# A product of zeros at the end of each slot of PE, and a tile's v sum taken ahead of the next c

## The chip, the cores and the metric

The kernel runs on one core of a Trainium2 chip. The metric is the device time of one launch in microseconds (us). The engines are named as in the profile: PE multiplies matrices, DVE, ACT and POOL work on vectors, SP issues transfers. POOL issues the gathers of table rows here.

## What is computed

One layer of a decoder for 1024 tokens of width 1024: an input norm and projection, an RWKV-7 recurrence and a causal convolution side by side, gates and an output projection, then the part that moves most of the data, a feed-forward layer of single experts, a gate from a per-layer embedding, and a last norm.

```python
h = h + (g_r * o_r + g_c * o_c) @ w_out              # RWKV-7 and convolution, gated
c = rms_norm(h, norm_ffn_g)
# peer_ffn(c): 8 heads, 16 experts each = 128 selections for a token
idx, gates = top_k_product_keys(c @ w_q, sub_keys)    # 128 of 16384 experts
u = jnp.take(u_tab, ib, axis=0)                       # 128 rows of 1024 for each token
coef = gb * gelu(einsum('cd,ced->ce', xb, u))
h = h + einsum('ce,ced->cd', coef, jnp.take(v_tab, ib, axis=0))
h = h + sigmoid(rms_norm(h, ple_norm_g) @ ple_w_gate) * (p @ ple_w_proj)
return rms_norm(h, final_norm_g)
```

Each token reads 128 rows of u and 128 rows of v, 4 KB each: 1.07 GB in all.

## The kernel before

**Tiles, periods, slots.** The tokens are cut into 8 tiles of 128 (NT = 8). After a start phase the program runs periods t = 0 to 10 of 128 slots s each, on every engine in the same written order, held together by semaphores alone. A period works on three tiles at once:

- The u part of tile t. In slot s POOL gathers row s of all 128 tokens' selections (gather_u, L761, 512 KB) into a ring of five buffers (UR = 5), and DVE takes 128 dot products of it with c (dot, L1924). The gather into a buffer waits for the dot that used it last.
- The v part of tile t - 2 (LAG = 2). In slot s POOL gathers the 128 rows of one token (gather_v, L778, 512 KB) into a ring of six buffers (VR = 6), ahead of that slot's gather_u in the same queue. PE multiplies these rows with the token's coefficients (add_tokens, L1085).
- The mixers of tile t + 1 (front), laid out over the slots on PE, ACT and DVE. Slots 20 to 66 hold the recurrence: 30 steps, one each 1.5 slots, in each of which a small product of PE (L803, L816, L825, L830, L872 to L889) waits for a copy of ACT (L1213) or an operation of DVE (L1553 to L1571) that waits for the product before. Slots 74 to 88 hold the mixers' products (L908), slots 90 to 97 the output projection (L983), slots 104 to 115 the queries (L1001).

In periods 0 and 1 there is no v part; PE has the projection of the later tokens instead (L1155). In period 7 there is no front. Periods 8 and 9 have v parts only, four tokens at a time, with eleven buffers.

**A token's v product.** The accumulator acc is 128 x 1024 in PSUM and is seen as four strips of 32 rows. Weights are 128 x 32 (the coefficients of one token in one of 32 columns, zeros beside), so a product writes one strip. Slot j's first half of columns goes to strip j % 4, its second half to strip (j % 4) ^ 2; products on different strips can run beside each other. Each float32 product stands in the trace as two matmuls, so a slot's two products are four records, "x4". A product with start=False adds to what the strip holds. The last product of slot j raises s_vmm, for which gather_v of token j + 6 waits.

**The end of a tile.** summed (L1933) adds acc to the residual hh with three DVE operations. It waits for all 128 tokens of the tile (s_vmm), and PE's first product of the next tile waits for it (s_hh), since it overwrites acc. It stands behind the second dot of the period. make_c (L1818) makes the period's c from the front's results and stands ahead of the first dot; the dots wait for it.

**Names.** e_v, e_u, e_a_rstd: ring buffers (e_a_rstd is the fifth of the u ring); e_wd: weights of the v products; e_acc: the accumulator; e_arena, e_pd: the recurrence's operands and its PSUM; e_zero: a tile of zeros that ACT spreads between the weights (spread); e_ones: a tile of ones; e_hh: the residual; e_gbc, e_hc, e_cw: the convolution.

Of the kernel before, what the change touches and what calls it, by code (L numbers as in the profile page):

```python
# [17 lines left out]
P = 128  # L18
# [278 lines left out]
def tail_step(t, s):  # L297

    if t == NT - 1:
        m, k = divmod(s - TAIL_AT, TAIL_SPAN)  # L300
        return (m, k) if 0 <= m < EARLY_TAILS else None
    if NT <= t < NT + LAG and 10 <= s < 10 + TAIL_SPAN:
        return EARLY_TAILS + t - NT, s - 10
    if t == NT + LAG and s < TAIL_SPAN:
        return NT - 1, s
    return None


def trunk(nc, io, dram):

    with ExitStack() as ctx:
        def buf(name, shape, dt=F32):
            return ctx.enter_context(nc.sbuf_tensor(name, shape, dt))
# [89 lines left out]
        pick = buf("e_pick", [P, 2, TOPK])  # L403
        iot, ioti = buf("e_iota", [P, TOPK]), buf("e_iotai", [P, TOPK], mybir.dt.int32)
        ex, ssum = buf("e_exp", [P, PH, TOPK]), buf("e_ssum", [P, PH])
        zero = buf("e_zero", [P, QUARTER * LANES])
        idx = [buf(f"e_idx{i}", [P, NSEL], U32) for i in range(2)]
        fidx = buf("e_idxf", [P, NSEL])
        idxT = [buf(f"e_idxT{i}", [P, P], U32) for i in range(LAG + 1)]
# [381 lines left out]
        def _(pe):  # L791
# [273 lines left out]
            def add_tokens(n, j, together):  # L1065
# [8 lines left out]
                for h in range(D // HALF):  # L1074
# [3 lines left out]
                    for i in range(together):  # L1078
# [8 lines left out]
                        if h == D // HALF - 1:  # L1087
                            last.then_inc(s_vmm, 1)

            def front(n, s):  # L1090
                if s in (2, 5, 9):
                    prep(n, (2, 5, 9).index(s))
                r = rec_step(s)
                if r:
                    rec(2 * n + r[0], r[1])
                if s == MIX_AT:
                    conv_mean(n)
                if s == MIX_AT + 1:
                    y_mean(n)
                if s == MIX_AT + 2:  # L1100
                    conv_variance(n)
                if s == MIX_AT + 3:
                    y_variance(n)
                for k in range(2 * KT):
                    if s == product_slot(k):
                        (conv_product, y_product)[k // KT](n, k % KT)
                if MIX_AT + 24 <= s < MIX_AT + 24 + KT:
                    mixed(n, s - MIX_AT - 24)
                if s == MIX_AT + 35:
                    c_turned(n)  # L1110
                if MIX_AT + 38 <= s < MIX_AT + 38 + FIRST_HEADS:
                    queries(n, s - MIX_AT - 38)
                if s == MIX_AT + 41:
                    scores(n, 0)
                if MIX_AT + 42 <= s < MIX_AT + 42 + PH - FIRST_HEADS:
                    queries(n, (4, 5, 6, 7, 2, 3)[s - MIX_AT - 42])
                if s == NEXT_HEAD_AT + HEAD_SPAN - 4:
                    scores(n, 1)
# [41 lines left out]
            def tail(m, k):  # L1160
                if k == 1:
                    tail_turned(m)
                if 4 <= k < 4 + KT:
                    ple_gate(m, k - 4)
                if k == 13:
                    ple_proj(m)
# [18 lines left out]
            for t in range(NT + LAG + 1):  # L1185
                for s in range(SLOTS):
                    if t < BLOCKS:
                        for i in behind_products(t, s):
                            behind_product(t, i)
                    if 1 <= t <= NT and s == 8:  # L1190
                        coef_turned(t - 1)
                    if LAG <= t < NT + LAG:
                        together = LAST_TOGETHER if t >= NT else TOGETHER
                        if s % together == 0:
                            add_tokens(t - LAG, s, together)
                    if t < NT:
                        for h in range(2, PH):
                            if s == head_slot(h) - 4:
                                scores(t, h)
                        if s == HEADS_END + 2:  # L1200
                            indices_turned(t)
                    if t + 1 < NT:
                        front(t + 1, s)
                    if tail_step(t, s):
                        tail(*tail_step(t, s))

        @block.scalar
        def _(act):
# [208 lines left out]
            def places(q):  # L1417
                w = wd[q % 2][:, :].rearrange("p (i x) -> p i x", x=WROW)
                q %= NSEL // (QUARTER * LANES)
                return w[:, :, QUARTER * q:QUARTER * q + 32 * (LANES - 1) + 1:32]  # L1420

            def spread(n, q):
                if n * (NSEL // (QUARTER * LANES)) + q >= 2:
                    act.wait_ge(s_vmm, n * NSEL + (q - 1) * QUARTER * LANES)
                act.activation(places(q + 6), zero[:, :].rearrange("p (i g) -> p i g", g=LANES), ACT.Copy)
                act.wait_ge(s_coT, n + 1)
                act.activation(places(q), coefT[n % 2][:, :].rearrange("p (g s) -> p s g", g=LANES)[:, QUARTER * q:QUARTER * (q + 1), :],
                               ACT.Copy).then_inc(s_wd, 1)
# [107 lines left out]
        def _(dve):  # L1536
# [486 lines left out]
            for s in range(FRONT_SLOTS, SLOTS):  # L2023
                front(0, s)
            for t in range(NT + LAG + 1):
                if t < NT:
                    make_c(t)
                for s in range(SLOTS):
                    if t < NT:
                        dot(t, s)  # L2030
                        if 0 <= s - head_slot(1) - 8 < 6:
                            select(t, 1, s - head_slot(1) - 8)
                        if s < head_slot(1) + 8:
                            head(t, 1, s - head_slot(1))
                    if s == (1 if t < NT + LAG else 0) and t > LAG:
                        summed(t - LAG - 1)
                    if s == 3 and 1 <= t <= NT:
                        coefficients(t - 1)
                    if t < NT:
                        for h in range(2, PH):  # L2040
                            if head_slot(h) <= s < head_slot(h) + 8:
                                head(t, h, s - head_slot(h))
                            if head_slot(h) + 8 <= s < head_slot(h) + 14:
                                select(t, h, s - head_slot(h) - 8)
                        if s == HEADS_END:
                            less_max(t)
                            indices_out(t)
                        if s == HEADS_END + 4:
                            softmax(t)
                            token_indices(t)  # L2050
                    if t < BLOCKS and s:
                        for m in behind_done(t, s - 1):
                            if kind(m) in ("z", "conv"):
                                behind_out(t, m)
                    if t + 1 < NT:
                        front(t + 1, s)
                    if tail_step(t, s):
                        tail(*tail_step(t, s))
# [71 lines left out]
```

## Time and profile before

| | |
|---|---|
| median of 3 runs | 3707.59 us (3706.16 to 3715.51) |
| the profiled execution | 3706.03 us, span 3704.3 us |
| mean granted clock of PE | 0.841 of full |
| PE, DVE, ACT, POOL busy | 2755.3, 2368.4, 525.3, 1979.5 us |
| make_c (L1818) of tiles 0 to 7 starts at | 276.8, 609.5, 945.9, 1346.3, 1741.6, 2126.9, 2522.7, 2914.3 us |
| summed (L1933) of tiles 0 to 7 starts at | 1351.9, 1747.3, 2132.5, 2529.1, 2919.4, 3283.5, 3479.0, 3666.4 us |

The starts of make_c mark the periods. Periods 0 and 1 take 333 and 336 us, periods 2 to 6 take 400, 395, 385, 396 and 392 us, period 7 takes 369 us, periods 8 and 9 some 190 us each.

### The profile page before, as it was taken

To read this page: it belongs to the slowest core of one execution; us is meant where nothing else is said; L and a number is where in the kernel's file an instruction comes from. 1 tells how busy PE (TensorE), PEld (TensorE's weight loads), DVE (VectorE), ACT (ScalarE), POOL (GpSimd) and SP (SyncE) were. 2 spreads that over 40 slices of the span, in tenths; PEclk is the share of its full clock that TensorE was granted. 3 is DMA by queue.
4 is the path that set the end of the run, shared out by engine and by line. 5 is a ranking of instruction groups with operands and counts; after the bars stand their busy time and mean duration, and the time that the engine had idled before them with its cause. 6 is when DMAs were issued, how large, how long until landed. Compare 5 with 4: busy or idle time off the path is not lost.

```text
span 3704.3 us, 41438 instructions
## 1 busy us (share of the span) xinstructions
PE 2755.3 (74%) x15264; PEld 1272.2 (34%) x15264; DVE 2368.4 (64%) x6063; ACT 525.3 (14%) x1165; POOL 1979.5 (53%) x2093
## 2 busy tenths in 40 slices
PE   9988988998657766676567756775667777677877
PEld 7764655556233322332133213331333112111111
DVE  4549889888767677676867686768675665520000
ACT  3222112221101010111110011101110121110000
POOL 0003334334556666566656665666566666656663
PEclk9999999999767877787778867886788778779999
DMA  6538899889999999999999999999999999999995
GB/s 194 178 133 278 295 319 344 284 285 333 355 323 345 404 378 360 335 394 370 367 334 396 380 366 333 383 382 385 331 362 402 409 388 373 379 372 356 373 354 207
DMA packets 381194, 1253.76 MB, mean 338 GB/s; under 512 B 40384, under 2 KB 76480, under 8 KB 380224
## 3 DMA queue, kind: packets, MB, share of 16 engines
q0 software_dynamic: 294912, 1073.87, 77.6%
q1 hardware_dynamic: 83776, 176.20, 13.4%
q8 instruction: 120, 1.97, 0.2%
q10 hardware_dynamic: 2304, 1.05, 0.1%
q14 instruction: 82, 0.67, 0.0%
HBM read 1221.47 MB, written 29.49 MB: 338 GB/s over the span
## 4 chain that ended last, share of the span: by engine, by line
PE 19%; DVE 18%; another core or an unknown queue 15%; issue 11%; DMA 10%; POOL 8%; ACT 2%; SPq 0%; POOLq 0%; DVEq 0%; ACTq 0%
DVE e_u L1924 6%; PE e_acc L1085 6%; DMA e_v<-in_v_tab,e_idxT 5%; POOL e_v L778 4%; DMA e_u<-in_u_tab,e_idx 3%; PE e_pd L983 2%; PE e_acc L1155 2%; POOL e_u L761 2%; DVE e_gbc L1659 2%; PE e_pd L1001 2%; PE e_pd L803 2%; DVE e_a_rstd L1924 2%; PE e_pd L1054 2%; PE e_pd L908 1%
## 5 line engine op out<-in xcount | busy, mean ns | idle before, releaser
L1085 PE MATMUL e_acc<-e_v,e_wd 128*32 128x512 f32 x3636 | 1079.2, 762 | 397.8 <-DMA e_v<-in_v_tab,e_idxT 269.2
L761 POOL DMA_INDIRECT e_u<-in_u_tab,e_idx x820 | 797.2, 972 | 863.2 <-DVE e_dots L1924 412.8
L1924 DVE CUSTOM_DVE_ANT_0 e_u<-e_u,e_c 128x1024 f32<-128x1024 f32 x820 | 996.0, 1215 | 311.5 <-DMA e_u<-in_u_tab,e_idx 251.7
L778 POOL DMA_INDIRECT e_v<-in_v_tab,e_idxT x909 | 866.0, 953 | 613.2 <-issue 220.4
L1085 PEld LDWEIGHTS e_acc<-e_v,e_wd 128*32 128x32 f32 x3636 | 145.0, 120 | 976.4 <-DMA e_v<-in_v_tab,e_idxT 581.1
L1155 PE MATMUL e_acc<-e_v 128*128 128x384 f32 x1216 | 434.3, 501 | 24.7 <-DMA e_v<-in_w_in 16.6
L1659 DVE SCALAR_TENSOR_TENSOR e_gbc<-e_hc,e_cw,e_gbc 128x128 f32<-128x128 f32 x960 | 310.4, 344 | 1.9 <-issue 0.6
L1924 DVE CUSTOM_DVE_ANT_0 e_a_rstd<-e_a_rstd,e_c 128x1024 f32<-128x1024 f32 x204 | 247.8, 1215 | 73.4 <-DMA e_a_rstd<-in_u_tab,e_idx 63.1
L803 PE MATMUL e_pd<-e_arena 64*64 64x64 f32 x3584 | 168.8, 251 | 159.8 <-ACT e_arena L1213 70.8
L1155 PEld LDWEIGHTS e_acc<-e_v 128*128 128x128 f32 x1216 | 224.7, 193 | 178.2 <-issue 28.6
L761 POOL DMA_INDIRECT e_a_rstd<-in_u_tab,e_idx x204 | 198.3, 972 | 130.8 <-DVE e_dots L1924 87.7
L803 PEld LDWEIGHTS e_pd<-e_arena 64*64 64x64 f32 x3584 | 144.2, 160 | 306.6 <-issue 129.6
L1933 DVE TENSOR_TENSOR e_hh<-e_hh,e_acc 64x512 f32<-64x512 f32 (+1 forms) x24 | 16.4, 683 | 275.2 <-remote 139.5
L1213 ACT ACTIVATE e_arena<-e_pd 128x512 f32<-128x512 f32 (+1 forms) x192 | 90.4, 471 | 708.8 <-remote 345.4
L983 PE MATMUL e_pd<-e_w_out,e_actT 128*128 128x512 f32 x256 | 138.2, 671 | 35.4 <-DVE e_actT L1790 26.7
L1001 PE MATMUL e_pd<-e_actT,e_w_q 128*128 128x128 f32 x1024 | 143.6, 296 | 17.0 <-issue 8.7
L1001 PEld LDWEIGHTS e_pd<-e_actT,e_w_q 128*128 128x128 f32 x1024 | 133.0, 208 | 63.0 <-issue 48.4
L1129 PE MATMUL e_acc<-e_w_q,e_u 128*128 128x256 f32 x608 | 141.5, 386 | 3.4 <-DVE e_w_q L2008 3.4
L1085 PE MATMUL e_acc<-e_u,e_wd 128*32 128x512 f32 x368 | 121.7, 629 | 25.3 <-DMA e_u<-in_v_tab,e_idxT 16.2
L1054 PE MATMUL e_pd<-e_w_out,e_actT 128*128 128x512 f32 x256 | 125.8, 625 | 2.3 <-ACT e_actT L1261 2.3
L1129 PEld LDWEIGHTS e_acc<-e_w_q,e_u 128*128 128x128 f32 x608 | 114.5, 192 | 23.2 <-issue 5.2
L778 POOL DMA_INDIRECT e_u<-in_v_tab,e_idxT x92 | 86.7, 943 | 48.9 <-issue 23.7
(266 smaller groups left out, 2761.1 us busy)
## 6 DMA issues: line engine op xcount, KB each, us to landing
e_v<-in_w_in SPq DMA_DIRECT2D x76, 512.0 KB
e_u<-in_w_in SPq DMA_DIRECT2D x38, 512.0 KB, 3.7
e_v<-in_v_tab,e_idxT POOLq DMA_INDIRECT x909
e_u<-in_u_tab,e_idx POOLq DMA_INDIRECT x820
e_ring<-in_w_c SPq DMA_DIRECT2D x32, 256.0 KB
e_zb<-in_w_c SPq DMA_DIRECT2D x32, 256.0 KB
e_ring<-in_w_r SPq DMA_DIRECT2D x32, 256.0 KB
e_zb<-in_w_r SPq DMA_DIRECT2D x32, 256.0 KB
```

Source lines behind the costliest of these rows:

```text
L761: pool.indirect_dma_start(out=u[m % UR][:, :], out_offset=None, in_=io["u_tab"], in_offset=bass.IndirectOffsetOnAxis(ap=idx[n % 2][:, j:j ...
L778: pool.indirect_dma_start(out=v[i], out_offset=None, in_=io["v_tab"], in_offset=bass.IndirectOffsetOnAxis(ap=idxT[n % (LAG + 1)][:, k:k + ...
L803: last = pe.matmul(pi[r, out, i * CH:(i + 1) * CH], a[r, i, :], b[r, i, :] if len(b.shape) == 3 else b[r, :], start=True, stop=True)
L983: last = pe.matmul(pd[:, h * HALF:(h + 1) * HALF], mixt[:, k, :], w_out[:, k, h * HALF:(h + 1) * HALF], start=(k == 0), stop=(k == KT - 1))
L1001: last = pe.matmul(pd[:, h * P:(h + 1) * P], w_q[:, k, h * P:(h + 1) * P], actT[:, k, :], start=(k == 0), stop=(k == KT - 1))
L1054: last = pe.matmul(pd[:, h * HALF:(h + 1) * HALF], actT[:, k, :], w_ple[:, k, h * HALF:(h + 1) * HALF], start=(k == 0), stop=(k == KT - 1))
L1085: last = pe.matmul(acc[rows, cols], w[:, at_:at_ + 32], v[v_place(m)[0]][:, cols], start=(step == 0), stop=True, skip_group_check=True)
L1129: last = pe.matmul(out, w_a[m % UW][:, k, :], ahead[:, k, :], start=(k == 0), stop=(k == KT - 1))
L1155: last = pe.matmul(acc[:, m % 2 * HALF:m % 2 * HALF + BEHIND_T], w_b[m % 2][:, k, :], behind[:, k, :], start=(k == 0), stop=(k == KT - 1))
L1213: act.activation(dst, src, ACT.Copy).then_inc(s_ra, 1)
L1659: dve.scalar_tensor_tensor(out=out, in0=hc[:, i, j:j + P], scalar=col(cw, j * CONV_TILES + i), in1=out, op0=ALU.mult, op1=ALU.add).then_in ...
L1924: dve.tensor_tensor_reduce(u[m % UR][:, :], u[m % UR][:, :], c[:, :], 1.0, 0.0, ALU.mult, ALU.add, dots[n % 2][:, j:j + 1]).then_inc(s_dot, 1)
```

## The change

Three things. keep_warm(s), a new function on PE, multiplies 32 columns of zeros with 512 columns of ones and adds the product to the strip s % 4, first half of columns, of acc. It runs as the last thing of slots 4 to 126 in periods 2 to 7: 738 times. It waits for nothing and raises nothing. The tile of zeros grows from 16 to 32 columns. And summed of the tile that is done moves on DVE from behind the second dot of a period to ahead of make_c.

```diff
-        zero = buf("e_zero", [P, QUARTER * LANES])
+        zero = buf("e_zero", [P, 32])
...
+            def keep_warm(j):
+                rows = slice(32 * (j % LANES), 32 * (j % LANES) + 32)
+                pe.matmul(acc[rows, 0:HALF], zero[:, :], ones[:, :].unsqueeze(1).to_broadcast([P, HALF // P, P]), start=False,
+                          stop=True, skip_group_check=True)
...
                     if tail_step(t, s):
                         tail(*tail_step(t, s))
+                    if LAG <= t < NT and LANES <= s < SLOTS - 1:
+                        keep_warm(s)
...
-                act.activation(places(q + 6), zero[:, :].rearrange("p (i g) -> p i g", g=LANES), ACT.Copy)
+                act.activation(places(q + 6), zero[:, 0:QUARTER * LANES].rearrange("p (i g) -> p i g", g=LANES), ACT.Copy)
...
             for t in range(NT + LAG + 1):
+                if t > LAG:
+                    summed(t - LAG - 1)
                 if t < NT:
                     make_c(t)
                 for s in range(SLOTS):
...
-                    if s == (1 if t < NT + LAG else 0) and t > LAG:
-                        summed(t - LAG - 1)
```

On PE, in the recurrence of a tile, the program stands in this order before (L803 a step of the recurrence, L1085 the v products, x4 or more where two or more slots follow each other with nothing between them; here one product is one row):

```order
L1085 MATMUL e_acc<-e_v,e_wd 32x512 x2
L803 MATMUL e_pd<-e_arena 64x64 x16
L1085 MATMUL e_acc<-e_v,e_wd 32x512 x4
L803 MATMUL e_pd<-e_arena 64x64 x8
L803 MATMUL e_pd<-e_m_id,e_arena 64x64 x8
L1085 MATMUL e_acc<-e_v,e_wd 32x512 x2
```

and now, the same stretch, with the new product as L1092:

```order
L1085 MATMUL e_acc<-e_v,e_wd 32x512 x2
L803 MATMUL e_pd<-e_arena 64x64 x16
L1092 MATMUL e_acc<-e_ones,e_zero 32x512
L1085 MATMUL e_acc<-e_v,e_wd 32x512 x2
L1092 MATMUL e_acc<-e_ones,e_zero 32x512
L1085 MATMUL e_acc<-e_v,e_wd 32x512 x2
L803 MATMUL e_pd<-e_arena 64x64 x8
L803 MATMUL e_pd<-e_m_id,e_arena 64x64 x8
L1092 MATMUL e_acc<-e_ones,e_zero 32x512
L1085 MATMUL e_acc<-e_v,e_wd 32x512 x2
```

Each slot's v products are followed by the slot's own other work and then by one product of zeros; where two slots' v products followed each other, a product of zeros now stands between them.

On DVE, at the start of a period, before (L1818 is make_c, L1924 a dot, L1933 the sum):

```order
L1849 MAX e_best<-e_onehot 128x8
L1818 SCALAR_TENSOR_TENSOR e_c<-e_x,e_stats,e_gt 128x1024
L1924 ISA e_u,e_dots<-e_u,e_c 128x1024
L1924 ISA e_dots 128x1
L1852 MAX_INDEX e_pos<-e_best,e_onehot 128x8
L1853 MATCH_REPLACE e_onehot<-e_best,e_onehot 128x256
L1597 TENSOR_TENSOR e_actT<-e_arena,e_vec 128x512
L1659 SCALAR_TENSOR_TENSOR e_gbc<-e_hc,e_cw,e_gbc 128x128
L1924 ISA e_u,e_dots<-e_u,e_c 128x1024
L1924 ISA e_dots 128x1
L1856 MAX e_best<-e_onehot 128x8
L1933 TENSOR_TENSOR e_hh<-e_hh,e_acc 128x512
```

and now (all lines of DVE stand 7 further on: L1825 is make_c, L1931 a dot, L1940 the sum):

```order
L1856 MAX e_best<-e_onehot 128x8
L1940 TENSOR_TENSOR e_hh<-e_hh,e_acc 128x512
L1940 TENSOR_TENSOR e_hh<-e_hh,e_acc 64x512 x2
L1825 SCALAR_TENSOR_TENSOR e_c<-e_x,e_stats,e_gt 128x1024
L1931 ISA e_u,e_dots<-e_u,e_c 128x1024
```

The three additions stand ahead of make_c and of the period's first dot.

## Rows read from the trace of the kernel before

**Rows 1.** The page: busy time, and PE's granted clock in 40 slices.

```profile
span 3704.3 us, 41438 instructions
PE 2755.3 (74%) x15264; PEld 1272.2 (34%) x15264; DVE 2368.4 (64%) x6063; ACT 525.3 (14%) x1165; POOL 1979.5 (53%) x2093
...
PEclk9999999999767877787778867886788778779999
```

**Rows 2.** Periods 1, 2, 5, 7: each engine's busy us, clock, DMA share, GB/s.

```profile
610.00:945.00 335.00, 299.06 (x1720) 188.88 (x1721) 286.91 (x744) 75.31 (x153) 119.62 (x124) 0.95 0.88 304
```

```profile
946.00:1346.00 400.00, 267.57 (x1626) 115.04 (x1626) 282.60 (x730) 45.08 (x104) 250.12 (x262) 0.76 0.97 361
...
2127.00:2523.00 396.00, 260.57 (x1626) 110.27 (x1626) 285.19 (x734) 44.22 (x101) 252.37 (x262) 0.78 0.98 367
...
2914.00:3284.00 370.00, 263.98 (x778) 64.45 (x778) 224.72 (x517) 52.11 (x114) 242.47 (x256) 0.77 0.99 382
```

**Rows 3.** The recurrence's stretches in periods 2 to 6, same columns.

```profile
1009.00:1171.00 162.00, 102.24 (x948) 50.89 (x944) 109.46 (x302) 16.41 (x40) 95.36 (x101) 0.71 0.92 330
...
2575.00:2733.00 158.00, 99.72 (x954) 46.93 (x951) 109.27 (x300) 16.42 (x40) 94.73 (x101) 0.75 0.95 343
sum 799.00, PE 502.03 PEld 242.73 DVE 545.71 ACT 81.84 POOL 476.81; mean PE 100.41 PEld 48.55 DVE 109.14 ACT 16.37 POOL 95.36
```

**Rows 4.** Two windows behind the recurrence, same columns.

```profile
1952.00:2003.00 51.00, 39.28 (x188) 19.75 (x188) 41.63 (x105) 7.22 (x13) 33.54 (x35) 0.84 1.02 391
```

```profile
2003.00:2027.00 24.00, 16.55 (x65) 6.38 (x64) 17.64 (x40) 0.00 (x0) 15.06 (x16) 0.78 1.03 409
```

**Rows 5.** Waits of 957 to 2914 us: total us, times, longest us.

```profile
PEld e_acc L1085 <- DMA e_v<-in_v_tab,e_idxT: 341.2, 146, 7.2
ACT e_arena L1213 <- remote: 339.1, 47, 15.0
...
DVE e_u L1924 <- DMA e_u<-in_u_tab,e_idx: 170.6, 142, 12.3
...
POOL e_v L778 <- PE e_acc L1085: 145.1, 102, 5.2
...
PE e_acc L1085 <- DVE e_hh L1933: 46.6, 4, 15.0
```

**Rows 6.** The same view of 277 to 945 us.

```profile
ACT e_arena L1213 <- remote: 6.3, 1, 6.3
```

**Rows 7.** PE in the recurrence of period 4: start, us, group, idle before and releaser.

```profile
1826.45 1.79 PE L803 MATMUL e_pd<-e_arena 64*64 64x64 f32 x32 [4.23 <-ACT e_arena L1213]
1828.17 1.92 PE L1085 MATMUL e_acc<-e_v,e_wd 128*32 128x512 f32 x4
1832.50 1.15 PE L803 MATMUL e_pd<-e_arena 64*64 64x64 f32 x32 [2.40 <-ACT e_arena L1213]
1833.58 1.94 PE L1085 MATMUL e_acc<-e_v,e_wd 128*32 128x512 f32 x8
```

**Rows 8.** PE in the output projection of period 5.

```profile
2437.60 1.05 PE L1085 MATMUL e_acc<-e_v,e_wd 128*32 128x512 f32 x4
2438.59 1.98 PE L983 MATMUL e_pd<-e_w_out,e_actT 128*128 128x512 f32 x4
2440.50 1.92 PE L1085 MATMUL e_acc<-e_v,e_wd 128*32 128x512 f32 x16
```

**Rows 9.** The change from period 4 to 5 on DVE.

```profile
2126.90 1.27 DVE L1818 SCALAR_TENSOR_TENSOR e_c<-e_x,e_stats,e_gt 128x1024 f32<-128x1024 f32 x1
...
2132.49 2.10 DVE L1933 TENSOR_TENSOR e_hh<-e_hh,e_acc 128x512 f32<-128x512 f32 x3
```

**Rows 10.** The same change of periods on PE.

```profile
2122.02 1.85 PE L1085 MATMUL e_acc<-e_v,e_wd 128*32 128x512 f32 x4 [0.64 <-DMA e_v<-in_v_tab,e_idxT]
2133.26 4.60 PE L1085 MATMUL e_acc<-e_v,e_wd 128*32 128x512 f32 x12 [9.39 <-DVE e_hh L1933]
```

## The prediction, made before the changed kernel was run

> **What bounds the kernel now.** I read the page first. No engine is full: PE is busy 74% of the span, DVE 64%, and PE's clock falls from full to seven or eight tenths once the slices of periods 0 and 1 are over [rows 1]. Then the windows by period: the DMA engines are busy 0.97 to 0.99 of the time in periods 2 to 7, at 361 to 382 GB/s [rows 2]. So the gathers nearly fill a full period. Windows inside a period show two kinds of stretch. Behind the recurrence the DMA moves 391 and 409 GB/s [rows 4], and I take 409 for the most it can do. In the recurrence (five stretches, 799 us in all) it moves only 330 to 343, mean some 338 [rows 3]. There something else sets the pace, and only there can a period still gain much: at 409 GB/s the same bytes would take 799 x 338/409 = 660 us, so 139 us is the most that all five could give.
>
> What sets the pace there is in the waits. PE's v products wait for rows of v, DVE's dots for rows of u, but POOL also waits 145.1 us for PE's v products to free buffers, and ACT waits 339.1 us for something that the view can't name ("remote"), up to 15.0 us at a time [rows 5]; in periods 0 and 1 that wait is 6.3 us [rows 6]. PE's program is in order. A step of the recurrence waits for ACT or DVE, and the v products behind it wait with it; then the ring of v stays full, POOL stands at gather_v, and gather_u behind it starves DVE. The timeline shows it: PE stands 4.23 and 2.40 us for ACT's copy, with the next slots' v products behind [rows 7].
>
> PE's clock has a part in this. In the stretches it is 0.71 to 0.75 [rows 3], that is, more than half of the work at the lower level of 1.2 GHz. A step of 32 products takes 1.79 us there and 1.15 at the upper level, one slot's v products 1.92 [rows 7] against 1.05 [rows 8]. In periods 0 and 1, where PE always has a product to do, the clock is 0.95 [rows 2].
>
> **The product of zeros.** It adds 738 products to PE, 123 in each of periods 2 to 7. Nothing of this form is in the trace. The nearest is half a slot's v products: the two halves lie on different strips, run beside each other and end after 1.05 us at full clock, 1.92 at half [rows 7, 8]. One product alone then holds its strip about as long as the pair: from 0.86 us (1.92 less 1.05 is the time that a second turn on the same strips adds [rows 8]) to 1.92. Where the next slot's v product follows at once it goes to other strips and may run beside it; where PE is idle anyway it costs nothing. It costs where the slot's own v product stands directly ahead of it with the strip still taken, and something is queued behind.
>
> Its gain is the clock. PE would have one more product in each slot of three us, mostly in the idle time after the slot's v products. Take period 4, 41 us from 1816: the groups of PE that stand ahead of or in a step of the recurrence and ran at half clock exceed their length at full clock by 0.6 to 0.9 us each (1.79 against 1.15, 1.92 against 1.05 [rows 7, 8]), and I count some six of them, 4.7 us. On a stretch of 160 us that is 18 us. Against it stand the new products that end up ahead of a step that is already released, 0.86 us each, some four in a stretch: 3 us. From the remaining 15 I take off 6, because the clock won't be full throughout and because part of the steps wait for ACT and DVE, whose operations don't get faster. Term: **9 us in each of five stretches, -45 us.** Bounds: 0 if the chain waits for other things, -139 by the DMA.
>
> Outside the recurrence I cost it at nothing. In the output projection PE is full at full clock, 2.9 us a slot [rows 8], but there the new product stands behind a product that goes to another accumulator, so it may run beside the next v products; the eight slots would cost at most 8 x 0.86 = 7 us a period, if it may not. In the remaining slots the DMA is at 391 to 409 GB/s [rows 4] and PE waits for v; a faster PE changes nothing. Period 7 has 382 GB/s already [rows 2].
>
> The Trainium skill ("TensorE: Matmul & The Clock Gate", Part 1) says that the array's clock is passed in two levels and that the gate follows how busy the array has been; of zeros as operands it says nothing there. Rows 2 and 3 agree as far as they go (0.95 with a busy PE, 0.71 to 0.78 with a waiting one); that a product of zeros on one strip of four counts, no row shows. By that rule the clock comes up, and the forecast stands; without it the third rival below holds.
>
> **The sum ahead of c.** DVE does the same three additions, 2.10 us, but before make_c and not 5.59 us later (2132.49 less 2126.90 [rows 9]). PE's first v product of the next tile waits for it: at this boundary PE was done at 2123.9 and began again at 2133.26, 9.39 us idle [rows 10]. This happens at five boundaries, 46.6 us in four of the waits [rows 5]. Meanwhile all six buffers of v are full, POOL stands at gather_v, and so the DMA. The sum now starts when DVE gets there, some 5.5 us sooner, and PE with it; c and the dots start 2.1 us later, which delays the release of u buffers by as much. The end of the wait moves from gather_v to the dots, but the u ring holds five gathers. Per boundary between +2 (only the delay counts) and -5.5 us (all of it counts); I take -3, since the DMA has some gathers of u in flight meanwhile. PE was done well before DVE comes to the sum, so the wait for s_vmm, which now stands ahead of make_c and every dot, ends at once. Term: **5 x -3 = -15 us.** (Bounds -27 and +10.) The larger tile of zeros costs nothing: ACT reads the same 16 columns.
>
> **Sum.** The profiled execution took 3706.0 us (span 3704.3), 1.6 below the median. 3706 - 45 - 15 = **3646 us**.
>
> **Rivals.**
>
> *A: only the move counts.* The clock rises, but the steps of the recurrence don't come sooner, since they wait for what ACT and DVE do and for signals that arrive late: ACT's unnamed waits of 339.1 us, 47 in five periods, against 6.3 in one [rows 5, 6]. For it: ACT is busy only 14% of the span, so it is not its work that is late, and a PE product whose record has long ended is what the copy waits for; a faster product shortens no such delay. Against it: half-clock groups do stand directly ahead of steps [rows 7]. Time: 3706 - 15 = 3691, and 3695 with a smaller gain by the move.
>
> *B: slower, by PE's turn in the catch-up.* After a wait of the chain PE has two to four slots of v products queued and does them side by side: two slots in 1.94 us [rows 7], four in 1.92 at full clock [rows 8], 0.48 each. Now a product of zeros stands between each two of them, on a strip that the one ahead of it still holds: 0.86 us more a slot. The catch-up is what frees the ring of v, for which POOL waits [rows 5]; if POOL starts 0.86 us later at each, the DMA loses it. In period 4's stretch I count 13 groups of two slots or more, some 16 such pairs a period: 5 x 16 x 0.86 = 69 us. It decides when PE's catch-up and not the chain's waits holds the gathers, that is, from the point where POOL's waits for L1085 grow beyond 145.1 us. Time: 3706 + 69 = 3775.
>
> *C: the change doesn't do what it says.* A product of zeros with one strip of 32 rows doesn't lift the clock. Then each costs up to 1.92 us at half clock [rows 7]: at rival B's 80 places 154 us, and with the move's 15 off 3706 + 139 = 3845 at most. With six tenths of it on the path, 3706 + 92 - 15 = 3783; I take some 3790.
>
> **How the numbers follow.** Forecast (the chain shortens with the clock): 0.40, 3610 to 3685. A: 0.21, 3685 to 3700. B: 0.33, 3715 to 3790, thinner in the first part. C: 0.06. What a measurement of this kernel can tell from no change is 0.3%, 11 us: 3696.5 to 3718.7. Faster is the forecast and most of A (the part of it where the move gives its full 15): 0.40 + 0.09 = 0.49. Same: the rest of A, and the lower rim of B: 0.12 + 0.04 = 0.16. Slower: 0.29 + 0.06 = 0.35. The range goes from the forecast's lower part to past B's middle, 3590 to 3785, leaving out C, the last third of B and a gain beyond 116 us by the unused DMA time: some 0.18 together. The forecast's own range is 3610 to 3685.
>
> **What would show it.** Clock: the granted clock in the five stretches above 0.9, and 32 products of L803 near 1.15 us, and one slot's v products near 1.05. If it stays at 0.71 to 0.75, C. Chain: the five stretches together at 755 us and 355 GB/s; if they stay at 799 with a high clock, A. Move: the idle time of PE at the five boundaries near 5 us in place of 9.39 and up to 15.0, and the wait of L1085 for the sum near 20 us in place of 46.6; the dots' wait for u at the start of a period not up by more than the 2 us. B would show as groups of v products and products of zeros that follow each other at 0.86 us or more, POOL's wait for L1085 above 145.1 us, and GB/s below 391 behind the recurrence. I would be wrong as well if the DMA, with both rings served better, moves less than 409 GB/s at its best, since then less than 139 us was ever to be had; and if the additions wait for the last v product of the tile, which would hold make_c and all dots behind it.

## The result

The changed kernel takes 3724.36 us (median of 9 runs, 3721.08 to 3732.32), the kernel before beside it 3707.59 us (9 runs, 3700.96 to 3715.72). The ratio is 1.0036, with a 95% interval of 1.0023 to 1.0048: slower by some 13 us by the ratio (17 us by the medians), where 61 us faster was forecast. The time lies in the range; the sign is wrong. Times and ratios here leave out three executions in a slower state, one of e12 and two of e16.

### The profile page after: what moved, and what is told of

It is laid out like the page before. It is cut to its first block, busy times and chain, and to the rows that moved or that the text cites. A ratio compares the mean times of both kernels' runs of the same rounds, so it can differ in the third digit from the quotient of the medians.

```text
span 3721.0 us, 44390 instructions
## 1 busy us (share of the span) xinstructions
PE 2899.6 (78%) x16740; PEld 1317.9 (35%) x16740; DVE 2365.9 (64%) x6063; ACT 526.1 (14%) x1165; POOL 1977.8 (53%) x2093
## 3 DMA queue, kind: packets, MB, share of 16 engines
q10 hardware_dynamic: 2304, 1.05, 0.1%
## 4 chain that ended last, share of the span: by engine, by line
PE 32%; DVE 20%; another core or an unknown queue 15%; DMA 13%; issue 9%; POOL 9%; ACT 2%; SPq 0%; POOLq 0%; ACTq 0%; DVEq 0%
DVE e_u L1931 6%; PE e_acc L1160 6%; POOL e_v L778 4%; DMA e_v<-in_v_tab,e_idxT 4%; DMA e_u<-in_u_tab,e_idx 4%; PE e_acc L1092 4%; PE e_acc L1085 4%; PE e_acc L1134 3%; PE e_pd L908 3%; PE e_pd L1001 3%; POOL e_u L761 3%; PE e_pd L803 2%; DVE e_gbc L1666 2%; PE e_pd L983 2%
## 5 line engine op out<-in xcount | busy, mean ns | idle before, releaser
L1085 PE MATMUL e_acc<-e_v,e_wd 128*32 128x512 f32 x3636 | 1063.0, 675 | 286.8 <-DMA e_v<-in_v_tab,e_idxT 186.9
L1931 DVE CUSTOM_DVE_ANT_0 e_u<-e_u,e_c 128x1024 f32<-128x1024 f32 x820 | 994.6, 1213 | 312.2 <-DMA e_u<-in_u_tab,e_idx 221.1
L1092 PE MATMUL e_acc<-e_ones,e_zero 128*32 128x512 f32 x1476 | 797.5, 667 | 4.5 <-issue 4.3
L1085 PEld LDWEIGHTS e_acc<-e_v,e_wd 128*32 128x32 f32 x3636 | 167.4, 114 | 757.6 <-DMA e_v<-in_v_tab,e_idxT 422.6
L1931 DVE CUSTOM_DVE_ANT_0 e_a_rstd<-e_a_rstd,e_c 128x1024 f32<-128x1024 f32 x204 | 247.5, 1213 | 66.0 <-DMA e_a_rstd<-in_u_tab,e_idx 47.5
L803 PE MATMUL e_pd<-e_arena 64*64 64x64 f32 x3584 | 152.8, 235 | 146.5 <-ACT e_arena L1220 79.5
L803 PEld LDWEIGHTS e_pd<-e_arena 64*64 64x64 f32 x3584 | 129.7, 146 | 273.8 <-ACT e_arena L1220 120.6
L1092 PEld LDWEIGHTS e_acc<-e_ones,e_zero 128*32 128x32 f32 x1476 | 134.7, 116 | 257.8 <-issue 234.9
L1940 DVE TENSOR_TENSOR e_hh<-e_hh,e_acc 64x512 f32<-64x512 f32 (+1 forms) x24 | 16.4, 685 | 284.1 <-remote 147.1
L1085 PE MATMUL e_acc<-e_u,e_wd 128*32 128x512 f32 x368 | 123.5, 644 | 26.7 <-DMA e_u<-in_v_tab,e_idxT 13.5
```

The costliest lines, as they stand in the source:

```text
L803: last = pe.matmul(pi[r, out, i * CH:(i + 1) * CH], a[r, i, :], b[r, i, :] if len(b.shape) == 3 else b[r, :], start=True, stop=True)
L1085: last = pe.matmul(acc[rows, cols], w[:, at_:at_ + 32], v[v_place(m)[0]][:, cols], start=(step == 0), stop=True, skip_group_check=True)
L1092: pe.matmul(acc[rows, 0:HALF], zero[:, :], ones[:, :].unsqueeze(1).to_broadcast([P, HALF // P, P]), start=False, stop=True, skip_group_che ...
L1931: dve.tensor_tensor_reduce(u[m % UR][:, :], u[m % UR][:, :], c[:, :], 1.0, 0.0, ALU.mult, ALU.add, dots[n % 2][:, j:j + 1]).then_inc(s_dot, 1)
```

## The profile after

The page first: PE has 1476 records more of weight loads and as many of products, and its clock is up nearly everywhere. The time isn't down.

```profile
span 3721.0 us, 44390 instructions
...
PE 2899.6 (78%) x16740; PEld 1317.9 (35%) x16740; DVE 2365.9 (64%) x6063; ACT 526.1 (14%) x1165; POOL 1977.8 (53%) x2093
...
PEclk9999999999878997898889988998888989999999
...
L1092 PE MATMUL e_acc<-e_ones,e_zero 128*32 128x512 f32 x1476 | 797.5, 667 | 4.5 <-issue 4.3
```

The windows of periods 2, 5 and 7, to hold against [rows 2] (us of the window, busy us of PE, PEld, DVE, ACT, POOL, then clock, DMA share, GB/s). The clock went from 0.76 to 0.78 up to 0.86 to 0.91; the GB/s did not move.

```profile
946.00:1350.00 404.00, 289.81 (x1874) 119.66 (x1874) 284.75 (x735) 47.31 (x109) 252.25 (x262) 0.86 0.96 360
2138.00:2530.00 392.00, 284.58 (x1873) 116.64 (x1872) 284.34 (x734) 44.05 (x101) 245.32 (x256) 0.88 0.97 365
2932.00:3298.00 366.00, 279.40 (x1023) 76.32 (x1022) 221.75 (x513) 50.06 (x112) 239.79 (x250) 0.91 1.00 382
```

The recurrence's stretches, against [rows 3]: the clock went from 0.71 to 0.75 up to 0.82 to 0.85, and the five took 808 us, not 799.

```profile
1008.00:1170.00 162.00, 107.90 (x1042) 48.27 (x1039) 108.86 (x300) 16.42 (x40) 95.45 (x101) 0.82 0.92 329
...
2581.00:2742.00 161.00, 106.46 (x1050) 45.92 (x1046) 109.21 (x302) 16.42 (x40) 95.07 (x101) 0.85 0.94 339
sum 808.00, PE 543.92 PEld 238.47 DVE 543.80 ACT 81.78 POOL 474.47; mean PE 108.78 PEld 47.70 DVE 108.76 ACT 16.36 POOL 94.89
```

The waits of 957 to 2914 us, against [rows 5]. PE waits far less for rows of v and for the sum (15.3 us in place of 46.6), POOL a little less for PE; ACT's unnamed wait is longer, 359.9 us in place of 339.1.

```profile
ACT e_arena L1220 <- remote: 359.9, 46, 15.9
...
PEld e_acc L1085 <- DMA e_v<-in_v_tab,e_idxT: 227.4, 131, 5.8
...
POOL e_v L778 <- PE e_acc L1085: 131.5, 98, 3.4
...
PE e_acc L1085 <- DVE e_hh L1940: 15.3, 3, 7.0
```

What such an unnamed wait is can be read at the change from period 4 to 5, first on PE, then on DVE. The tile's last v products are recorded from 2128.85 to 2129.90 us. DVE is free for the sum at 2133.48 and begins it at 2136.07, and c and the first dot stand behind it.

```profile
2128.85 1.05 PE L1085 MATMUL e_acc<-e_v,e_wd 128*32 128x512 f32 x4 [0.65 <-issue]
2136.87 4.63 PE L1085 MATMUL e_acc<-e_v,e_wd 128*32 128x512 f32 x12 [6.96 <-DVE e_hh L1940]
```

```profile
2133.06 0.42 DVE L1856 MAX8 e_best<-e_onehot 128x8 f32<-128x256 f32 x1
2136.07 2.12 DVE L1940 TENSOR_TENSOR e_hh<-e_hh,e_acc 128x512 f32<-128x512 f32 x3 [2.59 <-remote]
2138.23 1.29 DVE L1825 SCALAR_TENSOR_TENSOR e_c<-e_x,e_stats,e_gt 128x1024 f32<-128x1024 f32 x1
```

The semaphore that counts finished tokens has its last recorded rise at 2135.98 us, 6.1 us after the recorded end of the last product, and DVE starts 0.09 us behind it. So, as far as the recorded ends can be trusted (they are modelled), it is PE's **signal** that comes late, not its work. I measured this for all products of the mixers that raise a semaphore: the time from a product's recorded end to the rise that follows, where that is under 12 us (some rises are missing from a trace, so single values are rough). In the kernel before the median is 0.02 us in periods 0 and 1 (139 signals, mean 0.38) and 1.9 us in the five recurrence stretches (178 signals, mean 2.2), with 30 steps a stretch. The 0.08 us that the expectation of e3 names as the mean of periods 0 and 1 comes out only if everything over 1.5 us is left out. In the changed kernel the mean of the stretches is 2.25 us. ACT's copies in periods 2 to 6 show a median of 0.01 us, but only 114 of their 150 rises are recorded, against 158 of 160 of the products that they wait for.

A second place, behind the recurrence of period 5: the product of the convolution's variance (L942) is recorded to 2355.93. DVE, in order, is free for the next operation on it at 2358.15 and stands 2.01 us, until 2360.16, with dots behind.

```profile
2354.80 1.13 PE L942 MATMUL e_pd<-e_actT,e_ones 128*128 128x128 f32 x8 [1.20 <-ACT e_actT L1311]
```

```profile
2357.73 0.42 DVE L1856 MAX8 e_best<-e_onehot 128x8 f32<-128x256 f32 x1
2360.16 0.29 DVE L1680 TENSOR_SCALAR e_actT<-e_pd 128x128 f32<-128x128 f32 x1 [2.01 <-remote]
```

## The experiments

Ratios are to the kernel before, measured on the same chip; the chips differ (the kernel before has medians from 3687 to 3711 us), so times of different groups are not compared.

### Each half alone, and what makes the signals late

The move alone (no products of zeros):

```diff
-                    if LAG <= t < NT and LANES <= s < SLOTS - 1:
-                        keep_warm(s)
```

> The kernel before with the tile's sum ahead of the next c, without the products of zeros. The changed kernel measured 1.0036 of the kernel before. Theory S (the sum waits where it now stands): in the trace of the changed kernel DVE stands up to 2.59 us at the sum, with the last v product of the tile long recorded as ended (2129.90 us, the sum began at 2136.07), and c and all dots wait behind it; then the move alone gives +0 to +12 us. The prediction's term: -15 us. Rival: the move is worth nothing either way, within 3 us, and the whole +17 us belongs to the products of zeros.

Measured 0.9988 (0.9976 to 0.9999), 3686.09 against 3691.43 us: 5 us faster, a third of the term of -15, and not the +0 to +12 us of theory S. The wait it aims at is gone, and a smaller one stands on DVE (the sum's line in 1300 to 2945 us; before, PE waited 46.6 us [rows 5] and DVE never):

```profile
L1938 DVE TENSOR_TENSOR e_hh<-e_hh,e_acc x15: 670/686/690, 1343.9 to 2901.8; 64x512 f32<-64x512 f32 x10, 128x512 f32<-128x512 f32 x5
its engine sat idle before it (us, times) until:
  remote: 10.9, 3
who waited for it (us, times):
  PE e_acc L1085: 3.8, 1
...
```

The products of zeros alone, the sum where it was:

> The kernel before with the products of zeros, with the sum where it was. Theory L (steps of the recurrence wait for PE's signals, which come late by about 2 us whatever the clock is): granted clock up to about 0.91, recurrence stretches no shorter, +5 to +17 us. The prediction's term: -45 us. Rival B of the prediction (catch-up in PE's order): +69 us.

Measured 1.0028 (1.0015 to 1.0041), 3700.45 us, with the clock at 0.912. So the loss is theirs. The stretches took 794 us with the clock at 0.82 to 0.86, as theory L said.

A kernel whose v products read ones and wait for no gather (POOL waits instead until the gather before into the same buffer has landed, an edit that is not shown here):

```diff
-                            pe.wait_ge(s_v[v_place(m)[0]], 16 * v_place(m)[1])
...
-                        last = pe.matmul(acc[rows, cols], w[:, at_:at_ + 32], v[v_place(m)[0]][:, cols], start=(step == 0), stop=True,
+                        last = pe.matmul(acc[rows, cols], w[:, at_:at_ + 32], ones[:, :].unsqueeze(1).to_broadcast([P, HALF // P, P]), start=(step == 0), stop=True,
```

> A probe for what makes PE's signals late in periods 2 to 9. PE's v products read a fixed tile of ones and never wait for rows of v; the gathers are issued as before. (The sum over v is left out in this way.) In the kernel before, a product's signal comes 0.08 us on average after its recorded end in periods 0 and 1, but 1.99 us for the mixers' products in periods 2 to 6. If it is PE's waiting for gathers that holds the signals, they come within 0.1 us here, ACT's unnamed waits of 339 us fall below 100 us, and the time falls by some 100 us or more. If it is the v products themselves or the traffic, the signals stay at 1 to 2 us late and the time changes less than 60 us.

Measured 3686.15 us (one run). The mixers' signals are as late as before (2.1 us on average in the stretches), so PE's waiting for gathers doesn't hold them. It also says how little PE's readiness is worth: with v products that never wait for a gather, the time lies among those of the kernel before beside it, 3681 to 3699 us.

Each gather of v fetches 64 rows:

```diff
-                pool.indirect_dma_start(out=v[i], out_offset=None, in_=io["v_tab"],
+                some = P if m < VR else 64
+                pool.indirect_dma_start(out=v[i][0:some, :], out_offset=None, in_=io["v_tab"],
```

> The same probe from the side of the traffic: each gather of v fetches 64 of its 128 rows, in everything else the kernel before (half of the v rows are left out of the sum). If late signals come from DMA engines that are full, they go away with the traffic at three quarters, and the recurrence gets as fast as in periods 0 and 1. If they come from PE's waits for gathers or the v products, they stay at about 2 us, and periods 2 to 6 fall from some 393 us to no less than about 345 us, DVE's and the chain's own time.

Measured 4022.72 us (one run): slower, a period of 445 us at 254 GB/s, though with less to move. The DMA share is still about 1; why 64 rows are served worse was not followed, and neither branch of the expectation holds. The signals were less late all the same, 1.25 us on average in the stretches (183 signals, median 0.56), and ACT's unnamed wait halved (164.8 us over the five longer periods; the line is of 957 to 2914 us). Yet the slots 20 to 66 took no less time, 768 us in place of 766: here the slower gathers set the pace.

```profile
952.00:1397.00 445.00, 293.53 (x1626) 114.60 (x1626) 287.42 (x732) 46.66 (x107) 251.54 (x266) 0.73 1.04 254
```

```profile
ACT e_arena L1214 <- remote: 157.2, 23, 20.6
```

No gathers of v at all, with the v products on ones, and the same with the products of zeros:

```diff
-                pool.indirect_dma_start(out=v[i], out_offset=None, in_=io["v_tab"],
-                                        in_offset=bass.IndirectOffsetOnAxis(ap=idxT[n % (LAG + 1)][:, k:k + 1], axis=0)).then_inc(s_v[i], 16)
```

> The kernel before without the gathers of v; PE does the same v products on a fixed tile of ones (the sum over v is left out in this way). POOL still waits for each token's product before the next gather of u. It shows the chain of the recurrence without a full DMA. Theory L (PE's signals are late by some 2 us because the DMA engines are full): the signals come within 0.2 us, and the five recurrence stretches fall from 798 us to some 600 to 680. If the signals stay at 2 us, v products or PE's own order hold them, and the stretches stay above 750 us.

> The same as e11_no_v_gather with the 738 products of zeros. With signals prompt and no gathers of v, the chain alone is left, and what the clock is worth to it can be read: the prediction's term says -45 us or more in the five stretches against e11_no_v_gather. If the steps wait mainly for ACT and DVE, or the products of zeros take back what the clock gives, the two are within 15 us.

Without them 2936.85 us, 0.7920 (0.7907 to 0.7934). Signals come 0.33 us late on average in the stretches (172 signals, median 0.04), ACT's unnamed wait is nearly gone, and a stretch takes 109 us in place of 160, with DVE busy throughout:

```profile
1002.00:1112.00 110.00, 76.72 (x932) 41.04 (x932) 107.61 (x299) 15.92 (x39) 47.65 (x50) 0.84 0.76 237
...
sum 547.00, PE 381.73 PEld 201.82 DVE 539.48 ACT 79.61 POOL 238.18; mean PE 76.35 PEld 40.36 DVE 107.90 ACT 15.92 POOL 47.64
```

```profile
ACT e_arena L1208 <- remote: 15.0, 6, 2.7
```

This is the strongest finding: with the same products, and with the clock between 0.81 and 0.86, the chain of 30 steps fits into 109 us, less than the 120 to 136 that I expected, and the signals are late while the gathers of v run. How much of the 51 us a stretch is due to the signals is not shown, since half the traffic goes with them: at 409 GB/s the gathers of both tables alone would hold a stretch at 132 us (660 us in five, as in the prediction). With the products of zeros it is 2950.98 us, 0.7944 (0.7922 to 0.7965), and the stretches 550 us: nothing gained by the clock there either, where DVE is the bound. The two kernels ran on one chip, and the products of zeros cost 14 us by the medians (2940.25 to 2953.45 against 2936.43 to 2941.37 us), though DVE's unnamed waits came to 0 and 1.8 us. So at least the long ones have a price that needs no late signals.

### Where the products of zeros cost

In the recurrence alone, and in all other slots:

```diff
-                    if LAG <= t < NT and LANES <= s < SLOTS - 1:
+                    if LAG <= t < NT - 1 and 16 <= s < MIX_AT:
```

> Products of zeros in slots 16 to 65 of periods 2 to 6 alone (250 of 738), the sum where it was. In the traces of the changed kernel and of the products alone these stretches lasted 808 and 794 us against 798, with the clock up. Theory L (PE's signals come late in a full DMA, by about 2 us at either clock, so the steps come no sooner): within 5 us of the kernel before. The prediction's term: -45 us.

> Products of zeros in all the other slots (488 of 738), the sum where it was. Theory Q (the product of zeros takes its turn in PE's order, and where PE or the mixers' products pace the slots the gathers pay): the whole +10 us of the products alone appears here, most of it in slots 66 to 73 (117 us in place of 112.7 over five periods). The prediction: nothing, at most +7 us a period in the output projection. If the loss is spread evenly, +7 us.

Measured 1.0026 (1.0012 to 1.0041) and 1.0041 (1.0025 to 1.0057). A third of the products cost as much as all of them in e2 (1.0028), on another chip, and over half of what all cost in e15 below (1.0047). The parts add up to 1.0067; with intervals this wide, that is not clearly more than e15's whole. The part in the recurrence costs 7 to 10 us where theory L had under 5, and so the loss is not all in the other part, as theory Q had it.

Only behind other work of PE, and only directly between two slots' v products (rival B's place):

```diff
-                    if LAG <= t < NT and LANES <= s < SLOTS - 1:
+                    if LAG <= t < NT and LANES <= s < SLOTS - 1 and other_work(t, s):
```

other_work is true in the slots in which PE has anything to do behind the slot's v products; the second kernel has its negation.

> The sum where it was; products of zeros only in the 378 slots in which PE has other work after the slot's v products, so that none stands directly between the v products of two slots. Theory P (what costs is that a product of zeros keeps the v products of two slots from running side by side; the clock gives some of it back): the loss goes, -10 to +3 us against the kernel before. Rival I (each product costs a little wherever it stands, as an instruction or as time of PE): half of the +10 us or more, +5 to +10.

> The other half: products of zeros only in the 360 slots in which nothing stands behind the slot's v products, so that each stands directly between the v products of two slots. Theory P: the whole loss of the products alone and more, +12 to +30 us, since less clock is won. Rival I: +5 us.

Measured 1.0050 (1.0032 to 1.0068) and 1.0027 (1.0015 to 1.0040). I had expected the first to be harmless. It costs at least as much as the second (the intervals overlap): the price is not tied to the catch-up of v products, and theory P fell.

A quarter of the columns, and each product twice:

```diff
-                pe.matmul(acc[rows, 0:HALF], zero[:, :], ones[:, :].unsqueeze(1).to_broadcast([P, HALF // P, P]), start=False,
+                pe.matmul(acc[rows, 0:P], zero[:, :], ones[:, :], start=False,
```

> All 738 products of zeros, with 128 columns in place of 512, the sum where it was. Theory Q: the price follows PE's time, a quarter: +2 to +4 us, while the clock rises less. If the price is one of instructions (fetching, dispatching, signals) and not of PE's time, it stays at +10 us.

> Each product of zeros twice in a row, the sum where it was: the suspected price doubled. Theory Q: twice the +10 us or more, +20 to +60, since a slot's v products and two products of zeros take about 2.8 us where a slot has 3. If the +10 us came from something that goes with the clock alone (which is nearly full already), it stays at +10 us.

Measured 1.0064 (1.0045 to 1.0082) for the short ones, against 1.0028 for the long ones on another chip, and 1.0276 (1.0255 to 1.0298) for the long ones twice, 3811.05 us against 3711.13. Here theory Q fell for the short ones. The doubled ones cost 100 us, beyond what either theory gave; that PE's time counts there shows beside e17 below, where twice the tiny ones cost 1.0049.

### Presence, size and number

16 columns, 128 and 512, on one chip:

```diff
+                pe.matmul(acc[rows, 0:16], zero[:, :], ones[:, 0:16], start=False,
```

> All 738 products of zeros with 16 columns each, the sum where it was: the instructions are there, PE's time and the clock are not. Theory N (the price goes with PE's instructions and the signals they hold up; the clock gives back a part): +15 to +30 us, as the short ones or more, and the clock stays near 0.84. Theory Q (the price is PE's time): +0 to +3 us.

> The products of zeros with 128 columns once more, beside the tiny and the long ones on one chip. Theory N: +15 to +25 us again, no less than the long ones. If the +24 us of e7 was that chip's, it falls to +5 us or less.

> The products of zeros with 512 columns once more. Theory N: +8 to +14 us, less than the tiny and the short ones by what the clock gives back. Theory Q: more than both.

Measured 1.0044 (1.0027 to 1.0061), 1.0048 (1.0033 to 1.0063) and 1.0047 (1.0031 to 1.0063), with clocks of 0.851, 0.872 and 0.911 over the whole run. A product of 16 columns costs as much as one of 512, within intervals of some 6 us each way (theory N had 8 to 14 us for the long ones). So the price of the tiny ones is one of presence, not of time on PE. What the long ones add, time on PE and a higher clock, comes to nothing in sum; whether both are small or one pays for the other, no run separates.

The tiny ones twice, and the tiny ones in the kernel without gathers of v:

> 1476 products of zeros with 16 columns, two at the end of each slot, the sum where it was. Theory N (a price for each product that stands in PE's stream, whatever its size): about 1.009. If the price comes from a place where one more instruction of any kind puts a signal late, and no more by a second, it stays at 1.004 to 1.006. The long ones twice (e8) cost 1.0276; what lies between is then PE's time.

> The kernel without gathers of v (the sum over v is left out) with the 738 products of zeros of 16 columns. Without them it measured 0.7920 (0.7907 to 0.7934) of the kernel before, with those of 512 columns 0.7944. If the price needs the full DMA engines and its late signals, 0.7920 within 0.0015. If it is one of dispatch, 738 products at 20 ns, 15 us: 0.796.

Twice the tiny ones cost 1.0049 (1.0033 to 1.0066), no more than once: the price is not one for each product. The loading of PE's code is a rival that the traces can weigh. The queue of kind instruction, q8, moved 120 packets of 16 KB in the kernel before, 132 with 738 products of zeros, long or tiny, and 143 with 1476; e17 with its 143 costs no more than e13 with 132, and in periods 2 to 6 of the kernel before the mixers' signals were as late 20 us or more behind such a packet (mean 2.7 us, 87 signals) as within 4 us of one (2.5 us, 52). So neither the price nor the lateness follows the number of packets. Without gathers of v they take 2935.01 us against 2936.85 without any product of zeros, on different chips. The ratios (0.7957, 0.7938 to 0.7977, against 0.7920) differ because the kernel before took 3690 us on the one chip and 3707 on the other; whether a kernel without these gathers differs as much from chip to chip is not known. Whether the price of the tiny ones needs the late signals is therefore not decided by this pair: the ratios show a price, the times none of 15 us.

What the versions with products of zeros share shows in DVE's waits. I summed all unnamed ones ("remote") of DVE over periods 2 to 6. Without products of zeros: 164 us (before), 162 (move alone), 157 (e16), 154 (e3). With them, and the ratio behind: 168 (e2, 1.0028), 177 (e5, 1.0026), 184 (e10, 1.0027), 194 (changed kernel, 1.0036), 188 (e6, 1.0041), 197 (e13, 1.0044), 175 (e15, 1.0047), 192 (e14, 1.0048), 179 (e17, 1.0049), 232 (e9, 1.0050), 232 (e7, 1.0064). Without gathers of v: 0 to 2 us. Of these the two with the longest waits are the two dearest; e8, at 194 us and 1.0276, does not fit, and e4, without products of zeros, has 25 us. The line shown above, DVE L1680, is the clearest single place. In the kernel before, in e1 and in e16 it never waits for an unnamed releaser. In the changed kernel and in e7, in that order:

```profile
L1680 DVE TENSOR_SCALAR e_actT<-e_pd x5: 274/291/293, 1181.2 to 2754.3; 128x128 f32<-128x128 f32 x5
its engine sat idle before it (us, times) until:
  remote: 8.1, 4
```

```profile
L1680 DVE TENSOR_SCALAR e_actT<-e_pd x5: 290/292/293, 1179.8 to 2767.4; 128x128 f32<-128x128 f32 x5
its engine sat idle before it (us, times) until:
  remote: 15.7, 5
```

The signal that this line waits for came 0 to 1.3 us late in the kernel before, in e1 and in e16, and mostly 1.3 to 5.6 us late in those with products of zeros. So more instructions in PE's stream go with later signals at some places, and DVE pays. Over all signals of the mixers in periods 2 to 6 they don't clearly: 2.42 us on average in the kernel before, 2.22 to 2.76 with products of zeros. Each number is of one trace, and the order is loose in the middle; that the later signals are the price is argued and not shown, and the 14 us of the long ones without gathers of v (e12) speak against their being all of it.

### The sum between its two places

```diff
-                    if s == (1 if t < NT + LAG else 0) and t > LAG:
+                    if s == 0 and t > LAG:
```

> The kernel before with the tile's sum behind the first dot of a period and not behind the second; no products of zeros. Theory S (the sum can't start before the last product's signal, which comes 1.5 to 11 us after its recorded end): about half of the move's -4.5 us or all of it, since c and the first dot no longer wait: -2 to -6 us. The prediction's way of counting, 1 us for each boundary's 3 us earlier sum: -5 us.

Measured 0.9987 (0.9971 to 1.0003), 3682.07 against 3687.32 us. It is worth what the move ahead of c is worth, though its interval includes no change at all, and DVE stands only 0.8 us for PE's signal at the sum. The 6.0 us of issue stand once between the first addition and the second, where the program has no wait; their cause was not followed.

```profile
L1933 DVE TENSOR_TENSOR e_hh<-e_hh,e_acc x15: 675/682/691, 1349.8 to 2898.8; 64x512 f32<-64x512 f32 x10, 128x512 f32<-128x512 f32 x5
its engine sat idle before it (us, times) until:
  issue: 6.0, 1
  remote: 0.8, 1
who waited for it (us, times):
  PE e_acc L1085: 18.1, 3
...
```

## Why the prediction was wrong, step by step

**What bounds the kernel: half right.** That the DMA fills periods 2 to 7 outside the recurrence holds, and e3 agrees with it. That the chain sets the pace in the stretches is in part open: e11 brings them to 109 us, but takes away half the traffic with the late signals, and e4 has less late signals and stretches as long as before. That the clock had a part in the chain was wrong.

**The clock rises: right.** 0.82 to 0.85 in the stretches in place of 0.71 to 0.75, below the 0.9 that I named, v products at a mean of 675 ns in place of 762. The Trainium skill ("TensorE: Matmul & The Clock Gate", Part 1) says the gate follows how busy the array has been; by that rule a product of zeros counts like any other, and the trace agrees with these numbers. (That Part 1 says nothing of zeros as operands is too strong: it names them for another limit of the clock, not for this gate.) Rival C falls.

**The term of -45 us: wrong, it measured about 0.** The five stretches took 794 us (e2) and 808 us (the changed kernel) against 799. The step that failed is the count of half-clock groups "ahead of or in a step" as time of the chain, 4.7 us in 41. A step begins when ACT or DVE gets PE's signal, and that comes 2.2 us behind the recorded end on average at the lower clock, 2.25 at the higher. The rows were there: ACT's 339.1 us of unnamed waits [rows 5] against 6.3 [rows 6], which I gave to rival A with a chance of 0.21. Of the rivals A comes nearest in mechanism, and even it lacked a price for the products.

**"Outside the recurrence I cost it at nothing": wrong.** One product of zeros a slot costs 16 to 18 us (10 in e2, on another chip) whether it has 16 columns or 512 (e13 to e15); e6 has 1.0041 for the slots outside alone. I looked for its price in PE's time alone, between 0.86 and 1.92 us. What the price is made of stays open. Rival B had the sign right, but a price of 69 us and the wrong place: e10, with the products only where B sees them, costs 1.0027, e9, with none there, 1.0050.

**The term of -15 us for the move: right in sign, mis-sized.** It measured -5 us (e1, 0.9976 to 0.9999). PE's wait for the sum fell from 46.6 to 3.8 us in e1 and to 15.3 in the changed kernel, at least as far as I said. The step that failed is "PE was done well before DVE comes to the sum, so the wait ends at once": DVE stood 10.9 us in three of five changes of tile, since the last signal was late, and all dots with it. In the kernel before, DVE never stood at the sum: there c and two dots lie ahead of it. That the rest of the 15 us went since the gathers are bound by the DMA on both sides of the boundary is likely and not shown.

**The sum.** +10 (e2) to +17 (e15) for the products, whatever the clock gives back included, and -4 for the move (5 us by the medians) give +6 to +13, all by the ratios; measured +13, at the upper end. That the time lies in the stated range is luck: the range reached so far up for rival B, which had the sign but not the mechanism.

**Slips of the working.** 1.92 less 1.05 is 0.87, not 0.86, and 338 GB/s over 799 us are 358 GB/s over 755, not 355. The split of A does not fit its words: "most of A" gets 0.09 of 0.21. B's bounds are 3715 to 3790, so a range that ends at 3785 does not leave out its last third. None of these changes the forecast.

## What to carry to other kernels

Before pricing a faster engine, compare the end of its operation with the start of the one that waits for it: where a wait has no named releaser and the producer has long ended by the record, the signal is late, and a faster clock doesn't shorten that. A filler instruction is not free because its engine has gaps: try it at its smallest size too, and if that costs as much, its presence has a price of its own. A wait moved to the head of an in-order queue can show lateness that work ahead of it used to cover.

## What the runs showed of the hardware

While two streams of gathers kept the DMA engines full, the semaphore rises of PE's products in the recurrence came 2.2 us behind the recorded ends on average, up to some 10 us, and for the v products several at a time, 0.07 to 0.10 us apart (2135.81, 2135.91 and 2135.98 us for three tokens in the changed kernel, up to 11 us behind the recorded ends); without the gathers of v it was 0.33 us on average. ACT's recorded signals were prompt (median 0.01 us), with a quarter of them missing from the trace. PE's waiting for gathers plays no part by the trace of e3. What holds them, and why more instructions make it worse at some places, stays open; so does whether the recorded ends of the products are the true ones, and whether recording the trace has a part. And gathers of 64 rows ran at 254 GB/s in place of 361 and made the kernel 9% slower with 79% of the bytes (986.90 of 1253.76 MB).
